# The second layer's MLP as seven products for each pair of output tiles, with weight sums formed in DRAM

## The reference

```python
h2 = _rms_norm(x, lp['norm2_g']) * (1 + sc2) + sh2
x = x + g2 * (jnp.square(jax.nn.relu(h2 @ lp['w_ff1'])) @ lp['w_ff2'])
```

## Time and profile before

| what | us |
|---|---|
| median of 3 runs | 1906.96 |
| range of the runs | 1906.12 to 1909.41 |
| the profiled execution | 1910.12 |
| its span, first to last instruction | 1908.5 |
| TensorE busy | 1814.3 |
| DVE, ACT, POOL busy | 1066.0, 705.0, 464.3 |
| first layer's MLP | about 530 to 978 |
| second layer's MLP | 1433 to 1887 |

### The profile page before, as it was taken

How to read it: one execution, slowest core, us unless ns; L and a number is a source line. 1 busy time by engine, 2 the same in 40 slices (tenths; PEclk the granted TensorE clock), 3 DMA queues, 4 the chain that set the end, 5 groups by cost and what they waited for, 6 DMA issues and landing times. The chain is left out here.

```text
span 1908.5 us, 32411 instructions
## 1 busy us (share of the span) xinstructions
PE 1814.3 (95%) x13863; PEld 1722.1 (90%) x13863; DVE 1066.0 (56%) x1639; ACT 705.0 (37%) x1125; POOL 464.3 (24%) x334
## 2 busy tenths in 40 slices
PE   5999999898999999999999999889899999999996
PEld 3899976688999999999999998668899999999995
DVE  3687775567635676767655567556763323323233
ACT  2465346634341231312336533764433223131231
POOL 4000010144441230503530001105444113040244
PEclk9999999999999999999999999999999999999998
DMA  8653130111233444444132223002121221212211
GB/s 350 243 188 104 61 95 9 40 35 62 89 122 138 146 139 163 144 146 153 67 138 74 54 74 102 16 5 70 62 89 67 78 78 67 89 67 68 87 45 55
DMA packets 61147, 184.97 MB, mean 97 GB/s; under 512 B 21957, under 2 KB 34029, under 8 KB 45389
## 3 DMA queue, kind: packets, MB, share of 16 engines
q1 hardware_dynamic: 59468, 181.43, 27.6%
q10 hardware_dynamic: 1536, 1.48, 0.2%
HBM read 174.08 MB, written 8.72 MB: 96 GB/s over the span
## 5 line engine op out<-in xcount | busy, mean ns | idle before, releaser
L1655 PE MATMUL PS<-HH,HI 128*128 128x320 f32 (+1 forms) x1792 | 418.0, 315 | 5.2 <-DVE HL L1095 5.2
L1655 PE MATMUL PS<-HL,HI 128*128 128x320 f32 (+1 forms) x1792 | 413.2, 312 | 0.0
L1655 PE MATMUL PS<-HH,LO 128*128 128x320 f32 (+1 forms) x1792 | 411.1, 311 | 0.0
L713 ACT CAST HI<-RAW 128x2048 fp32r<-128x2048 f32 x96 | 182.7, 1903 | 470.7 <-PE PS L1655 444.1
L1655 PEld LDWEIGHTS PS<-HH,HI 128*128 128x128 f32 x1792 | 301.6, 190 | 5.8 <-issue 5.7
L1655 PEld LDWEIGHTS PS<-HL,HI 128*128 128x128 f32 x1792 | 306.8, 191 | 0.0
L1655 PEld LDWEIGHTS PS<-HH,LO 128*128 128x128 f32 x1792 | 303.9, 190 | 0.0
L1655 PE MATMUL PS<-FH,HI 128*128 128x320 f32 x1280 | 292.4, 310 | 5.5 <-issue 3.5
L1655 PE MATMUL PS<-FH,LO 128*128 128x320 f32 x1280 | 291.4, 309 | 0.0
L1088 DVE TENSOR_TENSOR LO<-RAW,HI 128x2048 fp32r<-128x2048 f32 x96 | 232.7, 2424 | 99.4 <-ACT HI L713 99.3
L1655 PE MATMUL PS<-FL,HI 128*128 128x320 f32 x1152 | 262.3, 309 | 0.0
(11 more groups left out here) (281 smaller groups left out, 2178.3 us busy)
## 6 DMA issues: line engine op xcount, KB each, us to landing
RAW<-ws SPq DMA_DIRECT2D x96, 1024.0 KB, 4.9
WM<-adt SPq DMA_DIRECT2D x48, 512.0 KB, 3.7
ADA<-ada SPq DMA_DIRECT2D x16, 1024.0 KB, 8.1
WMX<-adt SPq DMA_DIRECT2D x16, 512.0 KB, 3.8
EG<-gc SPq DMA_DIRECT2D x20, 256.0 KB, 3.9
X<-xT SPq DMA_DIRECT2D x1, 2560.0 KB, 15.6
X<-xT SPq DMA_DIRECT2D x2, 1280.0 KB, 5.8
xs<-X SPq DMA_DIRECT2D x1, 2560.0 KB, 8.0
```

Source lines behind the costliest of these rows:

```text
L713: nc.scalar.copy(HI[g % 2][:, :], RAW[g % 2][:, :]).then_inc(hi_ready, 1)
L1655: last = pe.matmul(bank(2 * u + a)[:, 0:e], w[:, cols], m[:, a * HT:a * HT + e], start=(k == 0 and f), stop=(k == KT - 1 and e_))
```

## The change

Only the second layer's MLP is computed in another way (`fast_mlp` in each engine's block). Two output tiles, two halves of the input features and the two token halves form a 2 x 2 by 2 x 2 block product, which is made with seven block products and additions instead of eight products. A pair of tiles is `p` (0 to 15 for w_ff1, 16 to 31 for w_ff2), a product is `w = 7p + i`. Each product is 4 feature blocks x 3 (high x high, high x low, low x high) = 12 matmuls of 322 columns in the first half, 320 in the second, all into one bank.

Three of the seven products read a block of the weights as it is, four read a sum or difference of blocks. These are formed in DRAM, in the new array `wp`, in the course of the first layer's MLP: SP issues 32 copies of 1 MB from `ws` to `wp`, and GpSimd issues 32 DMAs of 1 MB that add to `wp` (`weight_sum`). Each of these waits for the landing of the one before (sums_added) and, at the first of four, for a group of copies. They stand between GpSimd's steps for the hidden tiles 4 to 31, two behind the last hidden tile, one behind the last squares, and the 32nd at the beginning of the second layer, ahead of the clearing of QKV's columns.

Weight blocks of 256 KB go through eight slots (RAWB), are cast on ACT six products ahead and get their remainder on DVE five products ahead. The moving operand has seven blocks too (HB): made from X at the end of the projection by ACT and DVE for w_ff1. For w_ff2 the squared hidden tiles and their sums (four operations on GpSimd for each pair) are stored in DRAM (`hb`) and come back as seven blocks for each of four groups of pairs, split by ACT and DVE (five blocks) or GpSimd (two, `block_lo`). Taking out a pair costs DVE two sums (U2, U4) and four outputs (C11, C12, C21, C22); products 4, 6 and 7 add to banks that already hold one. In the second half C11 is added to X by DVE, the other three go through ACT (gate) to GpSimd (addition to X). The program's semaphores are lent: pp, on which the others wait for a product, is `gce`, wlo is `kde`, whi is `kdm`, c11 is `crb`, c12 is `chat`, c21 is `msq`, c22 is `mss`, e1 is `mke`, u2 is `mex`, u4 is `wi`, c22's readers fre and fsq are `mrb` and `map_`.

Some constants and tiles get other places in memory (SQA, YB, which becomes YF), and one of the prologue's semaphores is replaced. The core of the diff:

```diff
+FAST = (1,)
+PAIRS7 = 32
+HALF = PAIRS7 // 2
+PRODUCTS = 7
+SLOTS = 8
+BW = 328
+BX = HT + 2
+HI_AHEAD, LO_AHEAD = 6, 5
...
+        BANKS = (0, 3, 1, 0, 2, 3, 2)
+        PLAIN = {0: 0, 3: 1, 6: 3}
+        SUMMED = {4: 0, 1: 1, 2: 2, 5: 3}
...
+        VECTOR_BLOCKS, POOL_BLOCKS = (0, 1, 3, 4, 6), (2, 5)
+        STORED = (0, 3, 4, 1, 5, 2, 6)
...
+                    def weights_in(w):
+                        p, i = divmod(w, PRODUCTS)
+                        if i in PLAIN:
+                            src = t["ws"][g0 + p, 32 * PLAIN[i]:32 * PLAIN[i] + 32, :]
+                        else:
+                            src = t["wp"][SUMMED[i], p]
+                        sp.dma_start(RAWB[:, w % SLOTS, :], src.rearrange("r (a c) -> (r a) c", a=4)).then_inc(slot_in[w % SLOTS], 16)
...
+                    for w in range(7 * PAIRS7):
+                        if w + SLOTS < 7 * PAIRS7:
+                            sp.wait_ge(F["wlo"], b["wlo"] + w + 1)
+                            weights_in(w + SLOTS)
+                        p, i = divmod(w, PRODUCTS)
+                        if i == 5 and 2 <= p < HALF + 2:
+                            hidden_out(p - 2)
...
+                        if l + 1 in FAST and n < 13 + PAIRS7:
+                            g, kind = divmod(n - 13, 4)
+                            if g >= 2 and kind == 0:
+                                sp.wait_ge(sums_added, 16 * (4 * (g - 2) + 1))
+                            sp.dma_start(sums_of(4 * g, 4, kind),
+                                         blocks_of(g0 + CHUNKS + 16 + 4 * g, 4, STARTS[kind])).then_inc(sums_copied[g % 2], 16)
...
+                    def residuals(p):
+                        j = p % H
+                        for m, a in ((0, 1), (1, 1), (1, 0)):
+                            pool.wait_ge(F["gt"], b["gt"] + 2 * (p - HALF) + m + 1)
+                            y = X[:, j + H * m, a, :]
+                            nc.gpsimd.tensor_tensor(y, y, TMP[m][:, a, :], ALU.add).then_inc(F["xup"], 1)
...
+                    def block_lo(n):
+                        c, i = divmod(n, PRODUCTS)
+                        pool.wait_ge(F["fbh"], b["fbh"] + n + 1)
+                        nc.gpsimd.tensor_tensor(FB[i][:, 1, :, :], FS[n % 4][:, :, :], FB[i][:, 0, :, :].bitcast(F32),
+                                                ALU.subtract).then_inc(F["fbp"], 1)
...
+                def weight_sum(l, d):
+                    g, kind = divmod(d, 4)
+                    if kind == 0:
+                        pool.wait_ge(sums_copied[g % 2], 8 + 64 * (g // 2 + 1))
+                    if d:
+                        pool.wait_ge(sums_added, 16 * d)
+                    first = l * CHUNKS + 16 + 4 * g
+                    src = blocks_of(first, 4, 2 + kind) if kind < 2 else sums_of(4 * g, 4, kind - 1)
+                    nc.gpsimd.dma_start(sums_of(4 * g, 4, kind), src, accum_op=ALU.add).then_inc(sums_added, 16)
...
+                    if l in FAST:
+                        weight_sum(l, 4 * 8 - 1)
...
+                        if l + 1 in FAST and e >= 4:
+                            weight_sum(l + 1, e - 4)
+                    if l + 1 in FAST:
+                        weight_sum(l + 1, 28)
+                        weight_sum(l + 1, 29)
                     square_sum(2 * l + 2, updated(TILES - 8))
+                    if l + 1 in FAST:
+                        weight_sum(l + 1, 30)
...
+                    def weight_hi(w):
+                        act.wait_ge(slot_in[w % SLOTS], 16 * (w // SLOTS + 2))
+                        if w >= SLOTS:
+                            act.wait_ge(F["pp"], b["pp"] + w - SLOTS + 1)
+                        else:
+                            act.wait_ge(S["w_mm"], o["w_mm"] + PT_ + (6 if w < 4 else 8))
+                        nc.scalar.copy(WHL[:, w % SLOTS, 0, :], operand(w)).then_inc(F["whi"], 1)
...
+                    def weight_lo(w):
+                        dve.wait_ge(F["whi"], b["whi"] + w + 1)
+                        nc.vector.tensor_tensor(WHL[:, w % SLOTS, 1, :], operand(w),
+                                                WHL[:, w % SLOTS, 0, :].bitcast(F32), ALU.subtract).then_inc(F["wlo"], 1)
...
+                    def sums(p):
+                        n = BX if p < HALF else HT
+                        dve.wait_ge(F["pp"], b["pp"] + 7 * p + 3)
+                        if p:
+                            dve.wait_ge(F["c21"], b["c21"] + p)
+                        dve.wait_ge(F["e1"], b["e1"] + p + 1)
+                        nc.vector.tensor_tensor(U2[:, 0:n], bank(1)[:, 0:n], E1[:, 0:n], ALU.add).then_inc(F["u2"], 1)
+                        dve.wait_ge(F["u2"], b["u2"] + p + 1)
+                        nc.vector.tensor_tensor(U4[:, 0:HT], bank(3)[:, 0:HT], U2[:, 0:HT], ALU.add).then_inc(F["u4"], 1)
...
+                    def lower_right(p):
+                        dve.wait_ge(F["pp"], b["pp"] + 7 * p + 5)
+                        free(p, 1)
+                        nc.vector.tensor_tensor(TMP[1][:, 1, :], bank(2)[:, 0:HT], U4[:, 0:HT], ALU.subtract).then_inc(F["c22"], 1)
...
+                    def product(w):
+                        p, i = divmod(w, PRODUCTS)
+                        first, second = p < HALF, p >= HALF
+                        n = BX if first else HT
+                        pe.wait_ge(F["wlo"], b["wlo"] + w + 1)
+                        if p == 0 and i in (0, 2):
+                            pe.wait_ge(S["w_ev"], o["w_ev"] + PT_ + KT - 1)
+                        if p == 0 and i in (1, 4):
+                            pe.wait_ge(S["w_ev"], o["w_ev"] + PT_ + KT)
+                        if p == 0 and i in (0, 4, 6):
+                            pe.wait_ge(F["sxl"], b["sxl"] + {0: 1, 4: 2, 6: 3}[i])
+                        if i == 0 and p:
+                            pe.wait_ge(F["c11"], b["c11"] + p)
+                        if i == 1 and p:
+                            pe.wait_ge(F["c12"], b["c12"] + p)
+                        if i == 2 and p:
+                            pe.wait_ge(F["u2"], b["u2"] + p)
+                        if i == 3:
+                            pe.wait_ge(F["e1"], b["e1"] + p + 1)
+                        if i == 4 and p:
+                            pe.wait_ge(F["c21"], b["c21"] + p)
+                        if i == 5:
+                            pe.wait_ge(F["u4"], b["u4"] + p + 1)
+                        if i == 6:
+                            pe.wait_ge(F["c22"], b["c22"] + p + 1)
+                        if second and p % 4 == 0:
+                            c = (p - HALF) // 4
+                            name, own = ("fbp", POOL_BLOCKS) if i in POOL_BLOCKS else ("fbv", VECTOR_BLOCKS)
+                            pe.wait_ge(F[name], b[name] + len(own) * c + own.index(i) + 1)
+                        out = bank(BANKS[i])[:, 0:n]
+                        hi, lo = WHL[:, w % SLOTS, 0, :], WHL[:, w % SLOTS, 1, :]
+                        B = HB[i] if first else FB[i]
+                        opens = i in (0, 1, 2, 4)
+                        for k in range(H):
+                            if p == 0:
+                                pe.wait_ge(F["hbl"], b["hbl"] + {0: 2 * k + 1, 1: 2 * k + 2, 2: 9 + 4 * k, 3: 10 + 4 * k, 4: 11 + 4 * k,
+                                                                 5: 12 + 4 * k, 6: 25 + k}[i])
+                            cols = slice(k * P, (k + 1) * P)
+                            for v, (x, y) in enumerate(((hi, 0), (hi, 1), (lo, 0))):
+                                last = pe.matmul(out, x[:, cols], B[:, y, k, 0:n], start=(opens and k == 0 and v == 0),
+                                                 stop=(k == H - 1 and v == 2),
+                                                 skip_group_check=not opens)
+                        last.then_inc(F["pp"], 1)
...
+    for l in FAST:
+        w1 = a["w_ff1"][l].reshape(2, H, P, 4, 2, H, P).transpose(3, 5, 4, 0, 2, 1, 6)
+        w2 = a["w_ff2"][l].reshape(4, 2, H, P, 2, H, P).transpose(0, 5, 4, 1, 3, 2, 6)
+        ws[l, 16:] = np.concatenate([w1.reshape(16, P, KT * CH), w2.reshape(16, P, KT * CH)])
...
+    t["wp"] = nc.dram_tensor("wp", (4, PAIRS7, 32, KT * CH), F32, kind="Internal").ap()
+    t["hb"] = nc.dram_tensor("hb", (4, PRODUCTS, P, H, HT), F32, kind="Internal").ap()
```

More of the change, by code:

```diff
@@ L152, in build @@
         X = place("X", [P, KT, 2, HT], F32, r_x)
-        RAW = [place(f"RAW{i}", [P, KT * CH]) for i in range(2)]
+        r_raw = region(2 * KT * CH * 4)
+        RAW = [place(f"RAW{i}", [P, KT * CH], F32, r_raw + i * KT * CH * 4) for i in range(2)]
+        RAWB = place("RAWB", [P, SLOTS, H * P], F32, r_raw)
         r_split = region(4 * KT * CH * 4)
@@ L159, in build @@
         HL = place("HL", [P, KT, WS], F32R, r_h + KT * WS * 4)
-        YB = place("YB", [P, KT, 2, HT], F32, r_h)
         r_z = region(12 * CW * 4 + H * T * 4)
@@ L181, in build @@
         LW = place("LW", [P, 2, LEAF, LEAF], F32, r_x + 12288)
```

(13 more changed lines are left out.)

413 lines of the change are left out of this document (398 added, 15 removed).

## The result

The changed kernel takes 2001.5 us (median of 4 runs, 1998.9 to 2003.8) against 1907.2 for the kernel before on the same chip: 1.049 times, 95% interval 1.047 to 1.051. The forecast was 1879.0 with a range of 1857 to 1928. The time is outside the range, and the sign is wrong.

What follows compares the result with a forecast made beforehand. TensorE's matmul count was taken as the bound in the second layer's MLP. From 1910.1: -56.5 + 1 + 5 + 3 + 5.5 + 12 + 2.3 = 1882.4, less 3.1 for the runs' median: 1879 us, range 1857 to 1928.

Steps and rivals of the forecast that it cites:

- What bounds the kernel, matmuls removed, their price: Second layer's MLP: bound by the number of matmuls; 384 fewer at 0.147 us each save 56.5 us at most.
- Twelve matmuls in a row to one bank: Second layer's MLP: taken as free; a tenth more for each matmul would cost 39 us.
- GpSimd's queue as the place of harm, with next to no margin: First layer's MLP: FL steps queue behind waits for additions' landings, margin 0.3 us; cost put at 12 us.
- the second rival: First layer: slow additions make GpSimd's landing wait the bound; 1916 us at D = 10, about 1959 at 12; chance 0.25.
- D = 8.2: First layer: D, an accumulating DMA's time from issue to landing, taken as 8.2 us; no loss up to 7.5.
- The formula 6D - 45.2: First layer's MLP: lateness of the final FL step in each of three groups; 12 us in all.
- The layer boundary: Clearing QKV's pads stands behind the 31st addition's landing, delaying the norm turn: +2.3 us.
- 985 + D - 990.9: Layer boundary: pads ready at 985 + D against 990.9 needed; 2.3 us late at D of 8.2.
- The four splitting pairs, 1.25 us each: Second layer's MLP: where stored blocks are split, DVE makes C22 late; 4 x 1.25 = 5 us.
- the third rival: Second layer's MLP: DVE, slowed beside GpSimd, becomes the bound; 16 to 32 us, 1895 to 1911; chance 0.12 with dearer matmuls.
- The head: Start of the second layer's MLP: third product's block 1 us late, norm turn behind ACT and DVE; 3 us.
- The tail: End of the second layer's MLP: last product to norm sums 9.5 us instead of 4.11; +5.4, put at 5.5.

Runs made afterwards that it cites:

- experiment 1: Changed kernel with only the first of its 32 accumulating DMAs issued, all 32 copies kept: 1906.9 us, 1.0005 of the kernel before.
- experiment 3: Changed kernel with the same 32 additions spaced: behind every other hidden tile, or four in a row between groups; 1905.0 us, 0.9996 of the kernel before.
- Experiments 2 and 5: Each against the changed kernel: two additions in flight instead of one, 1950.9 us; each addition over half the bytes, 1941.4 us.
- experiment 9: Norm turn one product later, against the changed kernel with additions spaced and all block remainders on DVE (1888.4 us): 1885.7 us.

## Why the prediction was wrong

- **What bounds the kernel, matmuls removed, their price:** right. 384 matmuls at 0.147 went; 0.145 to 0.150 was found. Twelve matmuls in a row to one bank are not a tenth dearer; the first half's matmuls, all of 322 columns, cost about 3.5 us over 1344 x 0.147, where I had 1. I did not try what makes it.
- **GpSimd's queue as the place of harm, with next to no margin:** right. It is the second rival, with its mechanism.
- **D = 8.2 for every addition of a chain is the step that failed.** It measured 10.7 over the program and 10.8 to 12.3 in the group. The price of one addition by itself was right: the single one of experiment 1 landed in 8.2 us, and those 14.1 us apart (experiment 3) in 8.1 and 8.4. But I took this price for additions that follow each other every 7.05 us, and never asked whether all of them fit: by my own terms, 2 x 2.4 = 4.8 us of engine time in every 7.05 is a share of 0.68, and 0.5 was already taken. The sum is over 1 (measured: 1.34), so each addition gets what the others leave and D grows to 5.4/(1 - 0.57) = 12.6, an estimate that the four in a row of experiment 3 (12.1 to 12.8) bear out. Experiments 2 and 5 show the same from the other side: more in flight delays the rest, fewer bytes bring D down.
- **The formula 6D - 45.2** needs the whole round in D's place, some 1.4 us longer. With the measured 11.5 us it gives 3 x 23.8 + 5.8 = 77 us for the first layer; 82 were lost. So the formula held nearly (it has no term for the lower clock behind each wait; 63 of the 82 us are waits for FL), and the table of the second rival had 1959 for D = 12.
- **The layer boundary:** the mechanism was right, the size was again D. From the issue of the 31st addition to that of the 32nd it was 15.6 us, with which 985 + D - 990.9 gives 9.7; 11.1 were lost. Why this one takes longer than those in the group is open: X is stored beside it (2.5 MB, at 980 us in the kernel before too), and no run moved that.
- **The four splitting pairs, 1.25 us each, measured 8.3.** I had priced DVE's work there (17.9 us in 15.9) with GpSimd's block ahead of the residuals, but kept the doubling beside GpSimd for the third rival alone, as if it could only come in every pair. It came in exactly these pairs, and as more than a doubling: 0.68 became 3.40. And most of the waits took more time in lower clock, for which I had no term.
- **The head,** 3 us forecast, about 13 measured: two waits, 3.10 and 4.52 us, and a clock of 0.74 and 0.73 around them. With it the second layer's terms close: -56.5 + 3.5 + 33 + 13 = -7.0, measured -6.7. Only the second wait was tried (experiment 9), and its part of the 13 us not told from the clock's. **The tail,** 5.4 forecast, 5.2 measured.
- **Rivals.** The second came true, and the third in the four pairs. Their chances (0.25, 0.12) treated them as alternatives; here both occurred, in different stages, and the range took in neither sum.

## What to carry to other kernels

Before asking how long one DMA takes, add up the engine time of everything that stretch must move, with an accumulating DMA at about twice its bytes; over a share of 1 no order of waits helps, and below it the place in the issuing queue decides. The same 32 additions cost 94 us behind every hidden tile, and nothing when one stands behind every other tile and the rest in the idle stretches. A landing time that holds for one transfer alone doesn't hold for a row of them. A wait of TensorE of some 2 to 5 us is to be priced above its length here, since the clock behind it was lower for a while in most cases. And two changes that look independent in the sum (a step given to GpSimd, one added to DVE) can hold each other up: look at what runs at the same moment, in the pair where it is tightest, not at the mean.
